# Row sums of the spatial weights: from a matmul by ones on PE to a free-dimension reduction and square transposes on DVE

## What is computed

```python
def spatial_gating(z, ln_g, ln_b, w_s, b_s):
    u = z[..., :A_WIDTH]
    v = group_layer_norm(z[..., A_WIDTH:].reshape(bsz, s, A_GROUPS, A_GROUP_DIM), ln_g, ln_b)
    v = v.reshape(bsz, s // A_BLOCK, A_BLOCK, A_GROUPS, A_GROUP_DIM)
    w = jnp.where(block_causal_mask(A_BLOCK)[None], w_s, 0)      # 4 groups x 128 x 128
    gate = jnp.einsum('gts,bnsgd->bntgd', w, v) + b_s.T[None, None, :, :, None]
    return u * gate.reshape(bsz, s, A_WIDTH)
```

## Time and profile before

| | us |
|---|---|
| median of 3 runs (2091.25 to 2091.41) | 2091.39 |
| the profiled execution, its time | 2091.88 |
| its span in the profile | 2090.2 |
| granted TensorE clock, mean share of full | 0.999 |

### The profile page before, as it was taken

One profiled execution on the slowest core, in us unless ns is written; L12 is line 12 of the kernel. 1 busy time (PEld: TensorE's weight loads), 2 busy tenths in 40 slices (PEclk: granted clock), 3 DMA queues, 4 the chain that ended last, 5 costly groups with the idle time before them and its releaser, 6 DMA issues.

```text
span 2090.2 us, 29731 instructions
## 1 busy us (share of the span) xinstructions
PE 2077.9 (99%) x10934; PEld 1793.5 (86%) x10934; DVE 1577.1 (75%) x2005; ACT 1051.6 (50%) x1095; POOL 25.4 (1%) x57
## 2 busy tenths in 40 slices
PE   9999999999999999999999999999999999999998
PEld 7888888888888888888888888888888888888886
DVE  6888886777676776776787788997776677767677
ACT  7554564445444444455554554465454444444454
POOL 0000000000000000000010000000000000000000
PEclk9999999999999999999999999999999999999999
DMA  8645565555555655554665565556555556556552
GB/s 300 201 164 200 181 204 199 182 200 182 192 191 182 208 190 181 195 190 147 204 206 163 191 208 175 175 184 212 195 185 189 194 184 204 181 181 200 181 198 105
DMA packets 317188, 397.17 MB, mean 190 GB/s; under 512 B 8612, under 2 KB 240844, under 8 KB 317004
## 3 DMA queue, kind: packets, MB, share of 16 engines
q1 hardware_dynamic: 313500, 391.27, 56.0%
q0 software_dynamic: 1056, 3.16, 0.8%
q10 hardware_dynamic: 2576, 1.98, 0.3%
HBM read 394.28 MB, written 2.11 MB: 190 GB/s over the span
## 4 chain that ended last, share of the span: by engine, by line
PE 96%; DVE 1%; SPq 1%; issue 1%; ACT 1%; DMA 0%; DVEq 0%; ACTq 0%
PE ps_turned L1330 37%; PE ps_straight L1369 33%; PE ps_turned L1339 20%; PE ps_straight L1330 1%; PE ps_turned L1369 1%; PE ps_straight L1339 1%; DVE w_low L821 0%; DMA w_raw<-in_w_in_even 0%; PE ps_straight L1604 0%; ACT w_high L445 0%; PE ps_straight L1614 0%; SPq L288 0%; PE ps_straight L1489 0%; PE ps_straight L1624 0%; PE ps_turned L1565 0%
## 5 line engine op out<-in xcount | busy, mean ns | idle before, releaser
L821 DVE TENSOR_TENSOR w_low<-w_raw,w_high 128x2048 fp32r<-128x2048 f32 x369 | 844.6, 2292 | 348.0 <-ACT w_high L445 314.1
L445 ACT ACTIVATE w_high<-w_raw 128x2048 fp32r<-128x2048 f32 x368 | 704.0, 1917 | 662.2 <-PE ps_straight L1369 286.7
L1330 PE MATMUL ps_turned<-h_split,w_high 128*128 128x512 f32 x3456 | 802.8, 390 | 0.9 <-DVE work L998 0.9
L1330 PEld LDWEIGHTS ps_turned<-h_split,w_high 128*128 128x128 f32 x3456 | 643.6, 188 | 131.8 <-DVE work L998 1.3
L1339 PEld LDWEIGHTS ps_turned<-h_split,w_low 128*128 128x128 f32 x3456 | 425.1, 192 | 6.1 <-DVE w_low L821 0.2
L1339 PE MATMUL ps_turned<-h_split,w_low 128*128 128x256 f32 x3456 | 428.9, 283 | 0.0
L1369 PE MATMUL ps_straight<-w_high,y_split 128*128 128x512 f32 x1792 | 425.5, 390 | 0.4 <-DVE x L872 0.4
L1369 PEld LDWEIGHTS ps_straight<-w_high,y_split 128*128 128x128 f32 x1792 | 335.9, 188 | 70.3 <-issue 0.8
L1369 PE MATMUL ps_straight<-w_low,y_split 128*128 128x512 f32 x896 | 221.3, 389 | 0.0
L1369 PEld LDWEIGHTS ps_straight<-w_low,y_split 128*128 128x128 f32 x896 | 168.2, 188 | 34.9
L1058 DVE SCALAR_TENSOR_TENSOR work<-work,conv_columns 128x256 f32<-128x256 f32 x352 | 154.4, 480 | 12.2 <-DVE work L1058 2.5
(11 more groups left out here) (186 smaller groups left out, 756.1 us busy)
## 6 DMA issues: line engine op xcount, KB each, us to landing
w_raw<-in_w_up SPq DMA_DIRECT2D x176, 1024.0 KB, 5.0
w_raw<-in_w_down SPq DMA_DIRECT2D x88, 1024.0 KB, 5.0
w_raw<-in_w_in_odd SPq DMA_DIRECT2D x48, 1024.0 KB, 5.5
w_raw<-in_w_in_even SPq DMA_DIRECT2D x23, 1024.0 KB, 5.3
w_raw<-in_w_out_even SPq DMA_DIRECT2D x16, 1024.0 KB, 4.9
w_raw<-in_w_out_odd SPq DMA_DIRECT2D x16, 1024.0 KB, 5.0
work<-c_rows POOLq DMA_DIRECT2D x8, 256.0 KB, 6.5
x<-in_x SPq DMA_DIRECT2D x3, 512.0 KB, 11.1
```

The lines of the kernel that those rows point to most:

```text
L445: a.activation(wh[:, s, :], raw[:, s, :], ACT.Copy).then_inc(s_high, 1)
L821: ve.tensor_tensor(wl[:, s, :], raw[:, s, :], wh[:, s, :].bitcast(F32), ALU.subtract).then_inc(s_low, 1)
L1330: ins = pe.matmul(ps[:, 2 * slot + m, :], hi[:, kk, P * m:P * m + P], acts[:, K, :], start=(K == 0 and not narrow_ran), stop=(K == KC - 1) ...
```

## The change

DVE sums the untransposed weights `w_sp` (rows t, columns s) along the free dimension, in two instructions for the two halves of the mask, right after it has masked `WT`. The sums, one column for each group, go to `w_row`, four columns of `small`. In turn 7 `spread_over_rows` puts them on all rows of `WTsum`. PE's product by ones, DVE's copy out of `ps_turned` and the two semaphores around them go. PE now waits before the first pool piece for `s_WT`, the signal of the masking of `WT`.

```diff
--- before.py
+++ after.py
@@ -131,6 +131,7 @@
         vsum, vmu, vsq, vvar, vsd, vrr, vnt = (small[:, 24 + 8 * i:32 + 8 * i] for i in range(7))
         rmax, nmax, rsum, rinv = (small[:, 80 + 2 * i:82 + 2 * i] for i in range(4))
         cq = small[:, 88:152].rearrange("p (t h) -> p t h", t=2)
+        w_row = small[:, 88:92]
         inv_count = small[:, 120:136]
 
 
@@ -190,8 +191,6 @@
         s_cols = sem("columns_ready")
         s_spT = sem("spatial_turned")
         s_WT = sem("spatial_weights_ready")
-        s_wsum = sem("spatial_sums_done")
-        s_wsr = sem("spatial_sums_read")
         s_wp = sem("pool_product_done")
         s_turn = sem("x_turned")
         s_turn_hi = sem("turned_high")
@@ -925,6 +924,8 @@
                 ve.wait_ge(s_spT, 1)
                 link(ve.tensor_copy(WT, psT[:, 0, :].rearrange("p (g t) -> p g t", g=AG)))
                 fenced(ve.memset(WT[64:P, :, 0:64], 0.0), s_WT, 1)
+                ve.tensor_reduce(w_row[0:64, :], w_sp[0:64, :, 0:64], AX_X, ALU.add)
+                link(ve.tensor_reduce(w_row[64:P, :], w_sp[64:P, :, :], AX_X, ALU.add))
 
 
             ve.wait_ge(s_const, 4)
@@ -994,10 +995,10 @@
                 if n == 5:
                     spread_rstd()
                 if n == 6:
-                    ve.wait_ge(s_wsum, 1)
-                    fenced(ve.tensor_copy(WTsum, psT[:, 0, :].rearrange("p (g t) -> p g t", g=AG)), s_wsr, 1)
                     link(ve.memset(pp[:, :, 0:16], 0.0))
                     ve.wait_ge(s_bs, 16)
+                if n == 7:
+                    spread_over_rows(WTsum, w_row, AG)
                 if n == 8:
                     ve.wait_ge(s_z, 2)
                     fenced(ve.tensor_scalar(vmu, vsum, -1.0 / GD, None, ALU.mult), s_mu, 1)
@@ -1460,11 +1461,7 @@
                         for g in range(AG):
                             ins = pe.transpose(psT[:, 0, P * g:P * g + P], w_sp[:, g, :], ident[:, :])
                         ins.then_inc(s_spT, 1)
-                    if n == 6:
-                        pe.wait_ge(s_WT, 1)
-                        pe.matmul(psT[:, 0, :], ones[:, :], WT.rearrange("p g t -> p (g t)"), start=True, stop=True)\
-                            .then_inc(s_wsum, 1)
-            pe.wait_ge(s_wsr, 1)
+            pe.wait_ge(s_WT, 1)
             for j in range(4):
                 for k in range(2):
                     if j >= 2 and k == 0:
```

## The result

| | median us | lowest to highest | runs |
|---|---|---|---|
| before | 2091.40 | 2090.52 to 2092.57 | 22 |
| changed | 2094.74 | 2091.69 to 2097.41 | 22 |

The ratio is 1.0015 (95% interval 1.0008 to 1.0021): 3.3 us slower, where 1.3 were forecast. The changed kernel also scatters more: its runs cover 5.7 us, those of before 2.1 us. The mean granted clock, which is given to three digits only, is 0.999 in these three, 0.997 in 2096.01, 2096.47 and 2096.82 us, and 0.998 in the other sixteen. The profiled execution took 2094.77 us with a span of 2093.1.

A forecast was written before the change was run, and what follows sets the result against it. PE, busy for 99% of the span, bounds the kernel; DVE's lateness makes it wait 3.38 us, outweighing its 2.04 us gain by 1.34 us: 2091.39 + 1.34 = 2092.7 us, range 2091.5 to 2094.2.

The forecast's parts named there:

- The DVE part: DVE's queue up to low(19): reductions 1.10 us with fence, copy 0.76 us less, transposes 5.06 us; low(19) ends at 115.63 us.
- PE's gain: Up to the first pool piece PE gains 2.04 us, which drops out because DVE's chain sets the pool product's start.
- the idle time ahead of low(12): DVE's 4.58 us idle there is no room: it hangs on vmu through ACT, so low(12) moves by 4.71 us.
- Behind the product PE is the bound again: Through u and the output projection PE has no further wait, so the 1.34 us stays to the end.
- the clock falls in PE's new wait: Rival, chance 0.08: at the pool product PE's clock falls to half speed in the 3.4 us wait, giving 2096.4 us.
- The price of the fall: Clock rival's example: work behind the wait, as much as one group of 16 pool matmuls, takes 3.65 us more.
- the fixed part: At the pool product PE waits 3.38 us for low(19) and stands 1.34 us behind its old time.

The follow-up runs named there:

- the kernel with the product kept: Changed kernel, but PE still does the product by ones in turn 6, unread, waiting only for `s_WT`: 2092.37 us, ratio 1.0008.
- The two with the transposes behind vmu: Changed kernel with the sixteen transposes moved from turn 7 to just behind vmu in turn 8: 2089.03 us; the same with PE's unread product by ones: 2090.13 us.
- the filled kernel: Changed kernel, but PE does twelve unread products inside its wait for low(19) at the pool product: 2092.18 us, ratio 1.0004.
- the kernel with the longer wait: Changed kernel with the sixteen transposes done a second time, to the same place, right ahead of low(19): 2100.02 us, ratio 1.0041.
- the half-filled wait: Changed kernel, but PE does five unread products ahead of its wait for low(19) at the pool product: 2092.17 us, ratio 1.0005.

## Why the prediction was wrong

The DVE part held to 0.3 us. The reductions took 0.41 and 0.68 us (forecast 0.41 and 0.65), the transposes 5.04 us in their row and 5.07 us start to start (5.06), low(11) started at 66.71 us (66.42), vmu came at 68.92 us (68.63), low(19) ended at 113.63 + 2.29 = 115.92 us (115.63), PE started the product at 115.98 us (115.69) after 3.76 us of idle time (3.38). Some 0.2 us of those differences is that DVE was later already ahead of the change in this execution: the reductions start at 49.69 us, where low(8) stood at 49.48. A transpose took 0.315 us start to start, as the slope had it. The Trainium skill (VectorE: DVE Perf Modes, the TRN2 errata) has the formula of 58 cycles and one for each element, estimated as 0.19 us, and says further down in the same section that it comes out too short and that the measured fixed term is about 150 cycles; an estimate with that is 0.29 us. The prediction did not use the second figure. The trace is near it: the median length of the sixteen is 0.303 us.

That PE's gain drops out of the sum held too: in the kernel with the product kept PE comes to the pool product 0.8 us later and starts it 70.96 us behind the start of low(7), against 70.97 us without the product. The two with the transposes behind vmu show that the gain is real where DVE does not hold PE up.

That the idle time ahead of low(12) is no room for work ahead of vmu held as well. The same idle time is room for work behind vmu, which the prediction did not ask.

"Behind the product PE is the bound again", without a further wait, held in the changed kernel: the list of waits has none. It hung on what stands in DVE's queue there, as the kernel with the transposes behind the product shows. One hand-over ahead of the product was tighter than forecast. The stretch of pool matmuls from 85.92 to 97.29 us took 11.37 us, the like one behind it (to 108.41 us) 11.12 us; DVE's addition of that panel ended at 89.58 us, about when PE came to need it. That is argued from the times alone, and it drops out of the sum as PE's arrival does.

The step that failed is the clock. The prediction had "the clock falls in PE's new wait" as a rival with a chance of 0.08, because in the trace before the one fall came after 3.9 us of idle PE, and the wait would be 3.4 us. That took one long idle time for a bound from below. The runs show that shorter waits can be enough. With a wait of 3.76 us in the profile of the changed kernel, nineteen of its 22 runs lie above every run of the filled kernel, and all nineteen have a lower mean granted clock than the three others. With 2.08 us in the profile four of eleven runs lie apart in the same way, with 2.19 us two of eleven. With 0.7 us or with 1.2 and 0.5 us none does, and with 8.4 us all five do.

The price of the fall was off as well. The rival named 3.65 us for it, as an example (the 2.8 us beside it were the point from which a fall decides). The three profiles that have the fall around the pool product after a wait of 2.08 to 3.76 us lose 1.5 us each, and the one at the gates 1.7 us. Taken as the likely case with its own price, the fall would have put the forecast at 2096.4 us, 1.7 us over the 2094.74 measured; left among the rivals, it lay outside the range, which ended at 2094.2. The two errors offset each other in part: the clock added 2.4 us or more to the median, and the fixed part of 1.34 us was measured as 0.8 to 0.9 us.

Why the fixed part is smaller can be read in one pair of profiles. In all five kernels with the transposes in turn 7 and one wait at the product, PE starts the product 70.94 to 70.98 us behind the start of low(7) (with the second sixteen transposes, 5.08 us, taken off in the kernel with the longer wait). The forecast has 115.69 - 44.81 = 70.88 us. But low(7) itself started at 44.81 us in the profile of before, and between 44.14 and 45.01 us in those five. Where DVE's chain sets the time, this difference stays. Here are low(7) before, then low(7) and PE's start in the filled kernel:

```profile
44.81 2.29 DVE L821 TENSOR_TENSOR w_low<-w_raw,w_high 128x2048 fp32r<-128x2048 f32 x1 [2.45 <-ACT w_high L445]
```

```profile
44.44 2.29 DVE L820 TENSOR_TENSOR w_low<-w_raw,w_high 128x2048 fp32r<-128x2048 f32 x1 [2.45 <-ACT w_high L444]
115.38 0.50 PE L1487 MATMUL ps_straight<-y_split,w_high 128*128 128x512 f32 x1 [0.68 <-DVE w_low L820]
```

PE's start is 1.03 us behind its old time instead of 1.34, the first two products take 0.1 us more, and the wait for `x` of 0.38 us is gone. That leaves about 0.8 us, as the spans do (2091.0 - 2090.2).

What stays open: whether the medians differ for the same reason, why low(7) starts at different times, and why the medians give the fall of the clock 2.0 to 2.6 us where the profiles give 1.5. Three of the four slowest runs of the changed kernel have the lowest mean clock, 0.997, so the clock seems to stay low for longer in some runs than in the profiled one; no profile shows it.

## What to carry to other kernels

Work taken from the bound engine and given to one with idle time is a gain only if the receiving engine's queue has room at that place: an idle gap in front of an instruction is room only for work placed behind the event that ends the gap. Here the same sixteen instructions made the kernel 5.7 us slower than they did two instructions further on in DVE's queue, behind low(11) and vmu. And where a change makes PE wait in one piece, a fall of the clock has to be weighed: near 2 us it came in two to four of eleven runs here, at 3.76 us in nineteen of 22. There it belongs in the sum, not among the rivals. It also shows as scatter between runs, which is worth reading before the medians are compared.

## What the runs showed of the hardware

- The clock can fall after PE has started again. With waits of 2.08, 2.19 and 3.35 us it was full throughout the wait and fell some 0.4, 1.1 and 0.6 us behind PE's first matmul. The runs of one kernel differ in whether they pay for it: those of the kernel with the product kept fall into two groups about 2 us apart. The Trainium skill, TensorE: Matmul & The Clock Gate, section Why this matters for your kernels, tells to avoid longer idle gaps of PE between bursts of matmuls, and gives a return to the lower clock as the reason. The traces agree for 3.76 and 8.44 us; they also show that 2.08 and 2.19 us, less than the page names, were enough in some executions.
- What the lower clock costs follows from the work that stands behind the wait until it is full again: 1.5 us in the profile of the changed kernel, and as much with the half-filled wait (4.43 us for the first two products against 2.93) and with the product kept (4.44 us); 1.7 us at the gates, 2.4 us behind the longest wait.
